# A hybrid decoder trunk on one core: halves of the norm statistic, function tables, tile buffers and the place of the slab splits

## The reference, cut to what matters

```
def rmsnorm(x, w):   y = xf * lax.rsqrt(jnp.mean(xf * xf, axis=-1, keepdims=True) + EPS); return y * w
def modulate(h, shift, scale):  return h * (1 + scale[:, None, :]) + shift[:, None, :]
def swiglu(h, w_gu, w_down):    g, u = jnp.split(h @ w_gu, 2, axis=-1); return (jax.nn.silu(g) * u) @ w_down

h = modulate(rmsnorm(x, ffn_norm_w[i, 0]), sh1, sc1)
x = x + FFN_HALF * g1 * swiglu(h, ffn_w_gu[i, 0], ffn_w_down[i, 0])
h = modulate(rmsnorm(x, mix_norm_w[i]), shm, scm)        # then mamba2_mixer or swa_sink_attention
x = x + gm * y
h = modulate(rmsnorm(x, ffn_norm_w[i, 1]), sh2, sc2)     # then the second swiglu
```

## Time and profile before

| what | value |
|---|---|
| time, median of 3 runs | 2250.75 us (2249.43 to 2251.53) |
| the profiled execution | 2249.22 us, of which the span is 2247.3 |
| TensorE busy | 2152.0 us (96%) |
| VectorE busy | 1235.4 us (55%) |
| ScalarE busy | 848.4 us (38%) |
| granted TensorE clock, mean | 0.987 of full speed |
| read from device memory | 273.68 MB, 123 GB/s over the span |

### The profile page before, as it was taken

One profiled execution on the slowest core, in us unless ns is written; L12 is line 12 of the kernel. 1 busy time (PEld: TensorE's weight loads), 2 busy tenths in 40 slices (PEclk: granted clock), 3 DMA queues, 4 the chain that ended last, 5 costly groups with the idle time before them and its releaser, 6 DMA issues. The chain is left out here.

```text
span 2247.3 us, 28900 instructions
## 1 busy us (share of the span) xinstructions
PE 2152.0 (96%) x10542; PEld 1807.0 (80%) x10542; DVE 1235.4 (55%) x2024; ACT 848.4 (38%) x1235; POOL 9.2 (0%) x30
## 2 busy tenths in 40 slices
PE   4999999899999999899999989999998899999998
PEld 2888888788888878788888878888887778888887
DVE  6555466778887763655556653333345765333323
ACT  4333322554445542422222344443134645322212
POOL 0000000000000000000000000000010000000000
PEclk8999999999999999999999999999999999999999
DMA  7555576112211113455547522223322012223231
GB/s 296 202 191 194 176 249 236 63 57 85 66 65 65 57 57 106 150 186 199 199 173 251 181 75 93 93 93 103 113 94 66 1 47 85 93 93 101 96 112 66
DMA packets 77528, 276.80 MB, mean 123 GB/s; under 512 B 8592, under 2 KB 11152, under 8 KB 77328
## 3 DMA queue, kind: packets, MB, share of 16 engines
q1 hardware_dynamic: 77456, 275.81, 35.7%
HBM read 273.68 MB, written 2.10 MB: 123 GB/s over the span
## 5 line engine op out<-in xcount | busy, mean ns | idle before, releaser
L236 PE MATMUL bank<-h_hi,w_hi_sb 128*128 128x512 f32 (+1 forms) x1984 | 757.6, 382 | 41.4 <-DVE h_lo L369 27.6
L237 PE MATMUL bank<-h_lo,w_hi_sb 128*128 128x512 f32 (+1 forms) x1984 | 749.0, 378 | 0.0
L238 PE MATMUL bank<-h_hi,w_lo_sb 128*128 128x512 f32 (+1 forms) x1984 | 748.5, 377 | 0.0
L231 DVE TENSOR_TENSOR w_lo_sb<-raw,w_hi_sb 128x1024 fp32r<-128x1024 f32 x356 | 419.9, 1197 | 124.9 <-ACT w_hi_sb L226 120.7
L236 PEld LDWEIGHTS bank<-h_hi,w_hi_sb 128*128 128x128 f32 x1984 | 376.1, 190 | 119.5 <-issue 21.5
L237 PEld LDWEIGHTS bank<-h_lo,w_hi_sb 128*128 128x128 f32 x1984 | 376.3, 190 | 69.0 <-issue 1.7
L238 PEld LDWEIGHTS bank<-h_hi,w_lo_sb 128*128 128x128 f32 x1984 | 376.1, 190 | 68.5
L226 ACT ACTIVATE w_hi_sb<-raw 128x1024 fp32r<-128x1024 f32 x356 | 352.7, 1031 | 86.7 <-PE bank L238 85.9
L236 PE MATMUL bank<-a_hi,w_hi_sb 128*128 128x512 f32 (+1 forms) x792 | 290.1, 366 | 0.0
L237 PE MATMUL bank<-a_lo,w_hi_sb 128*128 128x512 f32 (+1 forms) x792 | 289.4, 365 | 0.0
L238 PE MATMUL bank<-a_hi,w_lo_sb 128*128 128x512 f32 (+1 forms) x792 | 289.4, 365 | 0.0
(11 more groups left out here) (200 smaller groups left out, 1880.7 us busy)
## 6 DMA issues: line engine op xcount, KB each, us to landing
raw<-w_stream SPq DMA_DIRECT2D x356, 512.0 KB, 4.4
mod_raw<-w_mod SPq DMA_DIRECT2D x144, 512.0 KB, 4.4
first_mod<-w_mod SPq DMA_DIRECT2D x16, 512.0 KB, 14.5
x_trunk<-x_in SPq DMA_DIRECT2D x1, 2048.0 KB, 10.5
trunk_out<-x_trunk SPq DMA_DIRECT2D x2, 512.0 KB, 3.0
trunk_out<-x_trunk SPq DMA_DIRECT2D x4, 256.0 KB, 2.1
c_row<-c_in SPq DMA_DIRECT2D x1, 512.0 KB, 4.2
att_rows<-att_rows_in SPq DMA_DIRECT2D x1, 136.0 KB, 4.5
```

The source lines that it names most:

```text
L231: nc.vector.tensor_tensor(w_lo_sb[:, s, 0:width], raw[:, s, 0:width], w_hi_sb[:, s, 0:width], ALU.subtract).then_inc(w_lo, 1)
L236: nc.tensor.matmul(ps, s_hi, m_hi, start=start, stop=False)
L237: nc.tensor.matmul(ps, s_hi, m_lo, start=False, stop=False)
L238: return nc.tensor.matmul(ps, s_lo, m_hi, start=False, stop=stop)
```

## The change

1. *Statistic.* `stat_after` goes from 7 (4 at the attention projection) to 3, so the statistic of half 0 comes behind four k steps of half 1. The statistic of half 1 is issued inside the first group of the next stage, before its k step 6, instead of behind it.
2. *Function tables.* The dummy logarithms go. `log_tables()` loads the logarithm's table at the start of each down projection and, for half 1, between tiles 3 and 4 of half 0; `silu_tables()` loads silu's ahead of the turns of a feed-forward stage, where the compiler had put loads into the loop.
3. *Three tile buffers.* In half-width norms the multiply goes round three quarters of `tmp` (the fourth is kept for the square); a multiply waits for the remainder three tiles back, not two.
4. *Splits.* Slab 1 is no longer split behind the square of half 0 but, at the three turn-overs that have `late=True`, behind tile 0 on ScalarE and behind the remainder of tile 1 on VectorE. The first splits of slabs 2 and 3 come behind tiles 5 and 6, the second splits behind all eight tiles.
5. *Key/value stage.* In the second norm the keys (L1066) and the first split of slab 4 come behind tile 4, that of slab 5 behind tile 5, with the second splits at the same places on VectorE; before, all of it stood behind tile 7.
6. *Second feed-forward stage, first turn.* VectorE finishes the second tile of the activation before it reads modulation blocks 2 and 3.
7. *Transfers.* In the turns with modulation blocks SP issues each slab load ahead of the block's, not behind it.

The core of the diff:

```
-        def use_pair_half(pe, b4, l, banks, m_hi, m_lo, hf, ready=None):
+        def use_pair_half(pe, b4, l, banks, m_hi, m_lo, hf, ready=None, stat=None):
             for k in range(8):
+                if k == 6 and stat is not None:
+                    stat_tensor(pe, stat, 1)
...
-            nc.scalar.activation(spare[:, 10 + st:11 + st], eps[:, 0:1], ACT.Ln)
...
+        def norm_tile(j, hf):
+            if hf is None:
+                return tmp[:, j % 2, :]
+            return (tmp[:, 0, half[0]], tmp[:, 1, half[0]], tmp[:, 1, half[1]])[j % 3]
...
-                if h0 + j > 1:
-                    dve.wait_ge(h_lo_ready, h0 + j - 1)
+                if h0 + j >= depth:
+                    dve.wait_ge(h_lo_ready, h0 + max(j - depth + 1, 0))
...
         def turn_over_scalar
             def between(j):
-                if j == 1:
-                    prep_hi(act, n1 // 4, 2)
+                if j == 0 and late:
+                    prep_hi(act, n1 // 4, 1)
+                if j == 3:
+                    log_tables()
                 if j == 4:
                     square_half(act, st, 1)
-                if j == 6:
-                    prep_hi(act, n1 // 4, 3)
+                if j in (5, 6):
+                    prep_hi(act, n1 // 4, j - 3)
...
         def turn_over_vector
             def between(j):
-                if j == 2:
-                    prep_lo(dve, n1 // 4, 2)
+                if j == 2 and late:
+                    prep_lo(dve, n1 // 4, 1)
...
             norm_vector(dve, st, hs, sh, hi, lo, 0, between)
+            prep_lo(dve, n1 // 4, 2)
             prep_lo(dve, n1 // 4, 3)
...
+        def log_tables():
+            nc.scalar.preload_act_table_set("natural_log")
...
         project_tensor / last_tile_tensor of the feed-forward stages
-                           lambda f: pe.wait_ge(a_lo_ready, ONE + FT * k + f + 1), st, 7)
+                           lambda f: pe.wait_ge(a_lo_ready, ONE + FT * k + f + 1), st, 3)
...
         ffn_vector, first turn
                     blocks(0)
+                    leave(1)
                     blocks(1)
-                    leave(1)
...
         kv_vector
-            norm_vector(dve, 3, 4, M_SH1B, h_hi, h_lo)
+            norm_vector(dve, 3, 4, M_SH1B, h_hi, h_lo, None, lambda j: prep_lo(dve, n4, j) if j in (4, 5) else None)
...
         gu_turn
+                            load_slab(sp, 4 * i + (n0 + 2 * u + q), (n0 + 2 * u + q) % RING)
                             if blocks:
                                 load_mod(sp, 4 * i + (m0 + 2 * u + q), q)
-                            load_slab(sp, 4 * i + (n0 + 2 * u + q), (n0 + 2 * u + q) % RING)
```

More of the change, by code:

```diff
@@ L473, in project_scalar @@
                     square_half(act, st, 0)
-                for l in late:
-                    prep_hi(act, n0 // 4, l, SLAB)
         def project_vector(dve, n0, spj, gate, st, last=False, mod0=None):
@@ L505, in project_vector @@
                     update_half(dve, bank[5], gate(j), 0)
-                for l in late:
-                    prep_lo(dve, n0 // 4, l, SLAB)
             if mod0 is not None:
@@ L1061, in kv_scalar, with between @@
             n4 = S_KV // 4
[L1062 to L1068 removed]
+            def between(j):
+                if j == 4:
+                    for l in range(2):
+                        act.wait_ge(slab_used, RING + S_KV + l + 1)
+                        b = COLS["b_k"][0] + l
+                        nc.scalar.activation(k_all[:, l, :], bank[l][:, :], ACT.Identity,
+                                             bias=cols[:, b:b + 1]).then_inc(k_ready, 1)
+                if j in (4, 5):
+                    prep_hi(act, n4, j)
+            norm_scalar(act, 4, M_SH1B, h_hi, None, between)
         def kv_vector(dve):
```

66 lines of the change are left out of this document (26 added, 40 removed).

## The result

The changed kernel takes 2236.3 us (median of 4 runs, 2234.62 to 2238.08), the kernel before beside it 2251.1: a ratio of 0.9934, 95% interval 0.9916 to 0.9951. Timed once more, with other runs beside it, it took 2236.4 and the ratio was 0.9940 (0.9927 to 0.9954). So it is faster by 14 to 15 us where 9.5 were forecast. The profiled execution took 2234.88 us with a span of 2233.1.

What follows compares the result with a forecast made beforehand. TensorE was taken as the bound, busy 2152.0 of 2247.3 us. Gains of 3.5 + 0.7 + 5.2 + 0.1 = 9.5 us took 2249.22 to 2239.7; the median, 1.5 higher, was forecast at 2241.2, range 2238.7 to 2243.7.

Steps and rivals of the forecast that it cites:

- first multiply: VectorE at the first turn-over: its first multiply starts at 399.5 instead of 402.58, 3.1 us sooner.
- the one gap before slab 5: Key/value stage: TensorE's idle time of 1304 to 1318 falls from 7.4 to about 3.3 us, one gap of 3.
- Turn-overs T1, T3, T4, T5: Gains at the first turn-over, into the key/value stage, before attention and behind attention: 0.8, 0.4, 1.2 and 0.2 us.
- step 2: First half of turn-overs: ScalarE's 8.8 us chain and the second splits use up most of the head start; turn-overs gain 3.5.
- Behind the state-space stage: Turn-over there, without the late split: the statistic comes 1.44 us sooner; gain 0.9 us taken.
- step 3: Start of the second feed-forward stage: activation tile first, slab 6 and function table fetched ahead; gain 0.7 us, 0 to 3.
- Step 4: Key/value stage: earlier second norm, with keys and splits between its tiles, lets TensorE reach slab 5 sooner; gain 5.2 us.
- rival (a): Clock stays up across the shorter key/value gap: 5.2 becomes 6.8, the 940 stretch gives 2 more; 2237.5 us, chance 0.13.
- Tail: End of the kernel: only the dummy logarithm leaves the path; gain 0.1 us.
- Rival (b): Head start lost and interlock: turn-overs give 1.5, key/value stage 4.2; gain 6.5 us, 2244.3, chance 0.14.
- Rival (c): Table loads between tiles cost 1.4 us more at each of five turn-overs; 2248.2 us, no difference, chance 0.08.
- Rival (d): Fetch order makes modulation blocks late in twenty loop turns, 1 us each; slower, 2261 us, chance 0.05.

Runs made afterwards that it cites:

- scalar_loaded_late: Changed kernel with two additional half-tile copies on ScalarE behind tiles 3 and 4 of each turn-over's first half; ratio 0.9953 to the kernel before.
- kv_only: Kernel before with nothing but the new ScalarE and VectorE order of the key/value stage; ratio 0.9995 to the kernel before.
- order_back: Changed kernel with the old fetch order and both modulation blocks again ahead of the second activation tile; ratio 0.9934 to the kernel before.
- splits_first: Changed kernel with both second slab splits ahead of the two modulation blocks in every gate/up loop turn; ratio 0.9908 to the kernel before.
- kv_back: Changed kernel with the old key/value order, keys and splits of slabs 4 and 5 behind all eight tiles of the second norm; 2236.8 us.
- after_again: The changed kernel unaltered, timed and profiled once more; 2236.4 us, ratio 0.9940 to the kernel before.
- scalar_loaded: Changed kernel with two additional half-tile copies on ScalarE behind tiles 1 and 2 of each turn-over's first half; ratio 0.9941 to the kernel before.
- split_back: Changed kernel with slab 1's split back behind the square of half 0 at three turn-overs; ratio 0.9944 to the kernel before.

## Why the prediction was wrong in size

Direction, logarithm, first multiply and the one gap before slab 5 were right. By term, forecast and measured (before less after in the profiled executions, second execution of after in brackets):

- Turn-overs T1, T3, T4, T5: 0.8, 0.4, 1.2, 0.2, measured 1.63, 1.07, 2.50 and 0.71, 5.9 instead of 2.6. This is the step that failed: the mechanism of **step 2** was right, its term for ScalarE's chain too large. It laid ScalarE's instructions one behind another by their durations, 8.8 us. From 399.99 to the end of tile 7 they occupy 9.68 less the pause of 1.68, so 8.0: but for the table load, each starts about 0.1 us before the one ahead of it ends. Tile 7's remainder ended at S' + 10.7, not S' + 11.6, and the rest of that sum, waits and hand-overs, came to 2.7 us where it had 2.8. scalar_loaded_late bears out that ScalarE's time from tile 3 on is passed on. The trace has the same at the other places: 8.0 us occupied by 8.8 of durations at T3 and T4, 7.1 by 7.8 at T5. At T4 it comes on top of GpSimd's pause. The last second split of half 0 ended 11.82 us after the first multiply there before the change, where it was 10.6 to 10.7 elsewhere, and 13.21 after it, against 12.98 at T1. So the chain of ScalarE absorbs all but 0.2 us of the pause, where I had taken 0.4 of 1.2.
- Behind the state-space stage and **step 3** together: 1.6, measured 0.6 (1.2). One trace cannot tell this term. The waits at slabs 6 and 7 came to 3.92 us in the first and 3.19 in the second execution of after, and to 3.46 in before and 4.73 in kv_only, which are alike up to there. Blocks still stood ahead of the splits, as I had it; order_back and splits_first show that their place on VectorE decides this stretch and the fetch order does not.
- **Step 4**: 5.2, measured 7.1 (5.8). The size was right but for the clock, and that part was luck: rival (a)'s 1.6 us came in the profiled execution and did not in the second. I had booked the head start within it at 3.1 less 0.3, and kv_back shows 3.2.
- Tail: 0.1, measured 0.1. Another 0.5 lies in the state-space stage and belongs to no change: from the transposes to the first output product it is 365.10 in before, 364.62 in after and 364.64 in kv_only, which is the kernel before up to there.

By its own figures ScalarE's chain in step 2 adds up to 8.7 and the difference in step 4 (1314.3 less 1309.0) is 5.3; neither changes the forecast by more than 0.1.

Rival (b), head start lost, did not come at its price; but the early statistic is paid back by the split between tiles, in a way that neither I nor (b) had priced. Rival (c), a further 1.38 us behind a table load, is refuted: the load at 404.46 takes 1.28 and tile 4 starts at 405.76. By an estimate from the figure of the Trainium skill ("ScalarE: Activation LUTs", "What ACT_TABLE_LOAD costs") it would have started at about 407.1. Rival (d) did not occur: T2+F, which holds ten loop turns with modulation blocks, is 358.76 with the old and 358.79 with the new fetch order.

## What to carry to other kernels

When engines hand over in turn, add up start-to-start distances from the trace, not durations, and find the pause: here 0.8 us of work ahead of it cost nothing, and the same work behind it cost 0.6 at T1, T3 and T4. Undo each part alone and also together with the part that relies on it: here the statistic cost 9.2 us and the split 1.9 when each went back alone, but only 4 to 5 when both did. Ahead of a wait for a transfer, do first what has already landed; two reordered lines gave 6.6 us, nearly half of what the whole change gave.

## What the runs showed of the hardware

The granted clock after one and the same gap is not fixed: with 2.5 us idle before slab 5 the stretch 1304 to 1318 ran at 1.00, 0.89 and 0.88 in after, after_again and order_back. KV tells the same of more executions: it is 259.55 in after, scalar_loaded and split_back, and 260.88 to 261.18 in after_again, order_back and splits_first, all with that same gap. So 1.3 to 1.6 us of such a term cannot be forecast, only bounded. And a wait can hide in busy time: T1 lost 1.63 us of length, but TensorE's idle time in the turn-over and before the closing transposes fell only from 2.64 to 1.77. In the kernel before, k steps of the first group that wait for a remainder start 0.92 us apart (409.28, 410.20, 411.12), where six products 0.12 apart take 0.72, and hardly any of that counts as idle.
